# A router fed by halves: rows normed with one product ahead of the root, modulation rows stored dealt, and a reordered opening

## The reference

```
mod = silu(c) @ ada_w[l] + ada_b[l]      # 6 rows: sh1, sc1, g1, sh2, sc2, g2
h = rmsnorm(x, norm_mix_g[l]) * (1 + sc1) + sh1
x = x + g1 * mixer(h)                    # l=0: LRU and convolution; l=1: attention
h = rmsnorm(x, norm_ffn_g[l]) * (1 + sc2) + sh2
scores = sigmoid(h @ router_w)           # 16 experts in 4 groups, top group, top 2
x = x + g2 * sum_e gate_e * expert_e(h)  # silu(h wg) * (h wu) @ wd
out = rmsnorm(x, final_norm_g)           # latent tokens only
```

## Time and profile before

| | |
|---|---|
| time, median of 3 runs | 993.85 us (991.39 to 996.26) |
| the profiled execution's own time | 990.79 us |
| its span, first to last instruction | 989.0 us |
| PE busy | 907.5 us (92%) |
| DVE / ACT / POOL busy | 389.2 / 255.1 / 112.7 us |
| moved by DMA | 314.32 MB, mean 318 GB/s |
| chain that ended last | PE 61%, DMA 25%, DVE 8%, ACT 4%, issue 2% |

### The profile page before, as it was taken

The page is one execution under the profiler, slowest core; times in us unless marked ns, Lnnn a source line. Parts: engine busy times, 40 slices in busy tenths (PEclk is TensorE's granted clock), DMA queues, the critical chain, the costliest instruction groups (busy, mean ns, idle before and its releaser), DMA issues.

```text
span 989.0 us, 14182 instructions
## 1 busy us (share of the span) xinstructions
PE 907.5 (92%) x5142; PEld 473.8 (48%) x5143; DVE 389.2 (39%) x815; ACT 255.1 (26%) x393; POOL 112.7 (11%) x220
## 2 busy tenths in 40 slices
PE   3899999999779999999999959999966999999996
PEld 1433343344336656565656615458423545555453
DVE  1389989833662222222222252665153111111112
ACT  3423446412321122111111132155031111111112
POOL 2300000100021111111111120000002111111110
PEclk9999999999979999999999989999977999999999
DMA  9992496667598899989999993782636999999994
GB/s 351 347 362 85 181 342 242 244 226 276 185 359 328 317 420 425 421 313 419 382 428 422 391 331 122 259 318 84 254 128 234 395 402 406 419 425 426 421 425 195
DMA packets 68116, 314.32 MB, mean 318 GB/s; under 512 B 4516, under 2 KB 4884, under 8 KB 51696
## 3 DMA queue, kind: packets, MB, share of 16 engines
q1 hardware_dynamic: 54608, 275.78, 70.5%
q0 software_dynamic: 8800, 29.75, 8.2%
q10 hardware_dynamic: 4672, 8.30, 2.4%
HBM read 299.35 MB, written 14.47 MB: 317 GB/s over the span
## 4 chain that ended last, share of the span: by engine, by line
PE 61%; DMA 25%; DVE 8%; ACT 4%; issue 2%; ACTq 0%; SPq 0%; DVEq 0%
PE ps L764 17%; PE ps L777 9%; PE ps L566 9%; PE ps L602 6%; DMA weight_ring<-in_exp_w_down 5%; DMA weight_ring<-in_exp_w_up 4%; DMA weight_ring<-in_exp_w_gate 4%; PE ps L495 3%; PE ps L873 3%; PE ps L835 3%; DMA hT<-in_exp_w_down 2%; DMA arena<-in_exp_w_gate 2%; DMA arena<-in_exp_w_up 2%; DMA weight_ring<-in_ev_w_in 2%; DMA weight_ring<-in_ada_w 2%
## 5 line engine op out<-in xcount | busy, mean ns | idle before, releaser
L764 PE MATMUL ps<-weight_ring,arena 128*64 128x256 f32 x1792 | 201.2, 382 | 4.8 <-issue 3.3
L764 PEld LDWEIGHTS ps<-weight_ring,arena 128*64 128x64 f32 x1792 | 141.1, 138 | 72.3 <-issue 21.6
L1344 DVE TENSOR_TENSOR arena<-arena,ps 128x128 f32<-128x128 f32 x78 | 18.9, 285 | 255.9 <-PE ps L764 255.9
L566 PE MATMUL ps<-hT,weight_ring 128*128 128x512 f32 x256 | 113.6, 597 | 1.5 <-DMA weight_ring<-in_ev_w_in 0.9
L777 PE MATMUL ps<-weight_ring,arena 128*64 128x512 f32 x448 | 102.3, 597 | 2.6
L1062 DVE SCALAR_TENSOR_TENSOR arena<-arena,par 128x512 f32<-128x512 f32 x132 | 95.0, 749 | 5.5 <-PE ps L566 1.6
L1727 ACT ACT_TABLE_LOAD x39 | 50.0, 1283 | 129.6 <-issue 129.3
L566 PEld LDWEIGHTS ps<-hT,weight_ring 128*128 128x128 f32 x256 | 47.4, 190 | 64.8 <-issue 63.0
L764 PE MATMUL ps<-arena 128*64 128x256 f32 x704 | 78.0, 379 | 0.0
L602 PE MATMUL ps<-weight_ring,arena 128*128 128x512 f32 x160 | 70.8, 595 | 0.7 <-DVE arena L1494 0.5
L764 PEld LDWEIGHTS ps<-arena 128*64 128x64 f32 x704 | 56.3, 137 | 24.4 <-issue 5.9
(11 more groups left out here) (315 smaller groups left out, 914.6 us busy)
## 6 DMA issues: line engine op xcount, KB each, us to landing
weight_ring<-in_ada_w SPq DMA_DIRECT2D x24, 2048.0 KB, 15.0
weight_ring<-in_exp_w_gate SPq DMA_DIRECT2D x22, 2048.0 KB, 10.1
weight_ring<-in_exp_w_up SPq DMA_DIRECT2D x22, 2048.0 KB, 10.4
weight_ring<-in_exp_w_down SPq DMA_DIRECT2D x22, 2048.0 KB, 11.0
arena<-in_exp_w_gate SPq DMA_DIRECT2D x10, 2048.0 KB, 10.4
hT<-in_exp_w_down SPq DMA_DIRECT2D x10, 2048.0 KB, 10.6
arena<-in_exp_w_up SPq DMA_DIRECT2D x10, 2048.0 KB, 11.0
weight_ring<-in_ev_w_in SPq DMA_DIRECT2D x4, 2048.0 KB, 19.3
```

Source lines behind the costliest of these rows:

```text
L566: last = mm(ps[:, m % 4, :], wide(slot)[:, k, P * j:P * j + P], hT[:, k, :], start=(k == 0), stop=(k == KD - 1))
L764: last = mm(ps[64 * fh:64 * fh + 64, bank, 0:256], xgT[:, k % 4, 64 * (k // 4):64 * (k // 4) + 64], w[:, k, 256 * fh:256 * fh + 256], star ...
```

## The change

**Router.** The norm's two passes change places and are cut in column halves. `times_gain` multiplies x by the gain row first (it needs no root): its left half before the product of the pass c=1 is awaited, its right half when that half of x is ready. The second pass is one instruction for each half, h times the inverse root plus shift, and each half has its own count on `s_h`. ACT squares the left half early (`left_squares`), puts that sum into the root's bias, and in `moe_rms` squares only the right half. PE transposes and ACT copies by halves. The last tile's logits go to bank 3, and all transposes of partial sums come after them. The table for the sigmoid is loaded before the last tile's copies.

**Rows.** sh2 and sc2 are copied by ACT and stored by POOL dealt already, in runs of 16 elements (64 bytes): five stores in layer 0 instead of one, three in layer 1 instead of one.

**Opening.** The root's table is loaded early, the context tiles are squared when they land, DVE squares the last tile, the second ada chunk goes to bank 5, and the transposes of x stand between the ada products in smaller groups.

```diff
             def rows_transpose(l, i):
                 t = toks(l)[i]
-                pe.wait_ge(s_h[l], i + 1)
                 if i:
-                    pe.wait_ge(s_h2[l], i)
-                for k in range(KD):
-                    last = tr(ps[:, 4 + k // 4, P * (k % 4):P * (k % 4) + P], hrow[:, t - CT * l, P * k:P * k + P], ident[:, :])
-                last.then_inc(s_h2m[l], 1)
+                    pe.wait_ge(s_h2[l], 2 * i)
+                for hf in range(2):
+                    pe.wait_ge(s_h[l], 2 * i + hf + 1)
+                    for k in range(4 * hf, 4 * hf + 4):
+                        last = tr(ps[:, 4 + hf, P * (k % 4):P * (k % 4) + P], hrow[:, t - CT * l, P * k:P * k + P], ident[:, :])
+                    last.then_inc(s_h2m[l], 1)
...
-                logits(0, n - 1, 1)
+                logits(0, n - 1, 6, 0)
                 rows_transpose(l, n - 1)
-                logits(n - 1, n, 2)
+                logits(n - 1, n, 3, 0)
+                logit_columns(0, n - 1, 1)
+                logit_columns(n - 1, n, 2)
...
+                        if c:
+                            ahead_of(i)
                         dve.wait_ge(s_op[l], m + 1)
...
+            def times_gain(l, i, gain, hf):
+
+                t = toks(l)[i]
+                dve.wait_ge(s_res[l], len(toks(l)) * hf + i + 1)
+                mark(v.tensor_tensor(in_blocks(hrow[:, t - CT * l, :])[:, :, 64 * hf:64 * hf + 64],
+                                     by_rows(x[:, t, 512 * hf:512 * hf + 512]),
+                                     in_blocks((mb, mb1)[l][gain])[:, :, 64 * hf:64 * hf + 64], ALU.mult))
+
             def moe_norm(l, i, gain, shift):
-                if i == 0:
-                    dve.wait_ge(s_nr, 64 + 32 * l)
                 t = toks(l)[i]
+                times_gain(l, i, gain, 1)
                 invert(rstd[:, 2 + l, t:t + 1])
-                h = in_blocks(hrow[:, t - CT * l, :])
-                link(v.scalar_tensor_tensor(h, by_rows(x[:, t, :]), rstd[:, 2 + l, t:t + 1], by_rows((mb, mb1)[l][gain]), ALU.mult, ALU.mult))
-                v.tensor_tensor(h, h, by_rows((mb, mb1)[l][shift]), ALU.add).then_inc(s_h[l], 1)
+                for hf in range(2):
+                    h = hrow[:, t - CT * l, 512 * hf:512 * hf + 512]
+                    v.scalar_tensor_tensor(h, h, rstd[:, 2 + l, t:t + 1], (mb, mb1)[l][shift][:, 512 * hf:512 * hf + 512],
+                                           ALU.mult, ALU.add).then_inc(s_h[l], 1)
...
+            def left_squares(l, i):
+
+                t, row = toks(l)[i], 2 + l
+                act.wait_ge(s_res[l], i + 1)
+                if i:
+                    act.wait_ge(s_ss[1 + 2 * l], 3 * i)
+                s.activation(sq_row[l][:, 0:512], x[:, t, 0:512], ACT.Square,
+                             accum_out=ss[:, row, t:t + 1]).then_inc(s_ss[1 + 2 * l], 1)
+                act.wait_ge(s_ss[1 + 2 * l], 3 * i + 1)
+                s.activation(ss_left[:, l, t:t + 1], ss[:, row, t:t + 1], ACT.Identity, scale=1.0 / D,
+                             bias=epsc[:, 0:1]).then_inc(s_ss[1 + 2 * l], 1)
...
+                        left_squares(0, i)
+                        if i:
+                            rows_columns(0, i - 1)
                         moe_rms(0, i)
...
             def router(l):
                 n = len(toks(l))
+                s.activation(att[:, 3, 0:1], epsc[:, 0:1], ACT.Sigmoid)
+                rows_columns(l, n - 1)
...
-            g.dma_start(mod_dram[0][:, 0:3].rearrange("v i (k n) -> (i k) v n", n=P), mod_rows[0].rearrange("p (v n) -> p v n", v=2)).then_inc(s_mst, 16)
-            pool.wait_ge(s_mst, 16)
+            g.dma_start(mod_dram[0][:, 0].rearrange("v (k n) -> k v n", n=P),
+                        mod_rows[0][0:8, :].rearrange("p (v n) -> p v n", v=2)).then_inc(s_mst, 16)
+            for i in (1, 2):
+                for w in range(2):
+                    g.dma_start(mod_dram[0][w, i].rearrange("(c k a) -> k c a", c=KD, k=KD),
+                                mod_rows_dealt[0][8 * i:8 * i + 8, P * w:P * w + P].rearrange("p (c a) -> p c a", c=KD)).then_inc(s_mst, 16)
+            pool.wait_ge(s_mst, 80)
```

More of the change, by code:

```diff
@@ L542, in half_ready @@
                 pe.wait_ge(s_hTa[1] if pair % 2 else s_hTd[1], 4 * half + 2 * (pair // 2) + k % 2 + 1)
[L544 to L551, removed]
+            ada_product(6)
+            ada_columns()
+            ada_product(5)
+            param_transposes()
+            ada_columns()
+            xn_transposes(0, 3)
+            ada_product(6)
+            xn_transposes(3, 5)
+            ada_columns()
+            xn_transposes(5, 6)
+            ada_product(6)
+            ada_columns()
             xn_transposes(6, KD)
@@ L1147, in _, with add_residual @@
                                        ALU.mult, ALU.mult).then_inc(s_nrm, 1)
-            def add_residual(l, tiles, bc_of, after):
+            def add_residual(l, tiles, bc_of, ahead_of, after):
                 n_t = len(tiles)
@@ L1188, in after_residual, with ahead_of_residual @@
                     moe_norm(0, i, *((2, 3) if i < CT else (4, 5)))
-            add_residual(0, range(NT), lambda t: 0 if cond_of(t) == CON else 1, after_residual)
+            def ahead_of_residual(i):
+                if i == 0:
+                    dve.wait_ge(s_nr, 64)
+                times_gain(0, i, 2 if i < CT else 4, 0)
+            add_residual(0, range(NT), lambda t: 0 if cond_of(t) == CON else 1, ahead_of_residual, after_residual)
             link(add_bias(0, 10, 12))
@@ L1549, in rms @@
                 s.activation(out, src, ACT.Sqrt, scale=1.0 / n, bias=epsc[:, 0:1]).then_inc(s_rms, 1)
-            act.wait_ge(s_x, 32)
-            squares(0, 0, range(NT))
-            rms(rstd[:, 0, :], ss[:, 0, :], D, 0, NT)
+            s.activation(att[:, 3, 2:3], epsc[:, 0:1], ACT.Sqrt)
+            act.wait_ge(s_ctx, 16)
+            squares(0, 0, range(CT))
+            act.wait_ge(s_x, 16)
+            act.wait_ge(s_ss[0], CT)
+            s.activation(junk, x[:, CT, :], ACT.Square, accum_out=ss[:, 0, CT:CT + 1]).then_inc(s_ss[0], 1)
+            act.wait_ge(s_pc, 2)
+            rms(rstd[:, 0, :], ss[:, 0, :], D, 0, NT - 1)
             ada = [0]
@@ L1647, in mod_rows_read @@
                 act.wait_ge(s_modT, l + 1)
-                s.activation(mod_rows[l], ps[0:(24, 8, 24, 8)[l], bank, 0:(2 * P, 2 * P, P, P)[l]], ACT.Copy).then_inc(s_mrow, 1)
+                read = s.activation(mod_rows[l], ps[0:(24, 8, 24, 8)[l], bank, 0:(2 * P, 2 * P, P, P)[l]], ACT.Copy)
+                if l in mod_rows_dealt:
+                    read = s.activation(mod_rows_dealt[l].rearrange("p (v k a) -> p v k a", k=KD, a=16),
+                                        ps[0:24, bank, 0:(2 * P, 0, P)[l]].rearrange("p (v a k) -> p v k a", k=KD, a=16), ACT.Copy)
+                read.then_inc(s_mrow, 1)
             mod_rows_read(0, 5)
@@ L1817, in _ @@
             prob_columns(2 * HEADS - 1)
+            left_squares(1, 0)
             moe_rms(1, 0)
+            left_squares(1, 1)
             rows_columns(1, 0)
```

102 lines of the change are left out of this document (62 added, 40 removed).

## The result

The changed kernel took 979.08 us (median of 4 runs, 978.45 to 980.43), the kernel before 993.15 us beside it (median of 4, 991.39 to 996.26): ratio 0.9867, 95% interval 0.9846 to 0.9887. The profiled execution took 978.45 us, with a span of 976.6 against 989.0.

What follows compares the result with a forecast made beforehand. PE bounds layer 0's experts, DMA and PE are level in layer 1, and both pay for the router's delay of the first tile. Terms 5.7 + 7.5 + 0 + 0 = 13.2 us took 993.85 to 980.6 us; range 972.5 to 988.

Steps and rivals of the forecast that it cites:

- Layer 0's router: From layer 0's last residual to the routing: L1222 at 266.1 instead of 271.8, a gain of 5.7 us, between 4.8 and 6.3.
- Step 2: Layer 0's router, ACT: Square of 512 columns with its sum takes 0.70 us, to 261.5; root 0.29, to 261.8.
- Step 3: Layer 0's router, DVE: right gain product from 260.19 takes 1.0 us and ends at 261.2, ahead of the root.
- Step 4: Layer 0's router: reciprocal with gaps 0.22 us, then contiguous passes of 0.69 each; halves of h at 262.75 and 263.45.
- Step 5: Layer 0's router: four transposes take 0.55 to 0.8 us; sigmoid's table loaded by 263.3; copies end at 264.0 and 264.8.
- Layer 1's router: In layer 1, L1222 starts at 730.8 to 731.6 instead of 738.67: gain 7.1 to 7.9 us, taken as 7.5.
- the reasons for more: Rival, gain 16 to 19 us: third chunk lands sooner, or PE stays at 2.4 GHz in layer 1; chance 0.06.
- the prediction's cold bound: Layer 1's router, lower end of the gain: 7.1 us, with eight transposes at 1.97 us cold instead of 1.09 warm.
- Opening: First ev_w_in product up to 1 us sooner, but the third chunk still lands at 52.8: gain 0, from -0.5 to +1.
- Rows stored dealt: Layer 0's five stores of 64-byte runs take 6 us, hidden, as the residual needs the rows ten us after they land.
- the late gather: Rival, layer 0's first tile: packed weight loads delay the gather past some 2 us of slack; gain 8 to 11; chance 0.20, shared with cold PE.

Runs made afterwards that it cites:

- the two kernels with the same router and colder transposes: The changed kernel with POOL's 13 small loads after the first ev_w_in product, 978.04 us; the same with one layer-0 weight load behind the gather too, 974.54 us.
- gather first: The changed kernel with the 2 MB load of expert 1's down weights in layer 0 issued after the first tile's gathered rows land: 976.47 us, ratio 0.9842.
- router alone: The changed kernel without its opening, so router and dealt rows on the kernel before: 979.86 us, ratio 0.9878.
- both repairs: The changed kernel with one layer-0 weight load behind the first tile's gather and POOL's thirteen small loads after the first ev_w_in product: 974.54 us, ratio 0.9822.
- all five kernels with a part put back: The changed kernel with one undone: early gain product 984.49 us, halved transposes and copies 983.37, early table 979.97, dealt rows 981.96, halved squares 980.38.
- old opening with late loads: The changed router and dealt rows with the opening of the kernel before, POOL's thirteen small loads after the first ev_w_in product: 977.66 us, ratio 0.9852.
- small loads late: The changed kernel with POOL's 13 small loads issued after the first ev_w_in product instead of the first modulation: 978.04 us, ratio 0.9865.

## Why the prediction was right, step by step

**Forecast.** 980.6 us for a measured 979.1; by the profiled executions 13.2 us forecast and 12.34 measured (990.79 less 978.45), by the medians 14.1.

**Layer 0's router** (5.7): 6.33 at L1262, 0.45 of it brought along from the last residual, 5.88 in the chain itself. Step 2 took 0.70 for the Square and its sum: 0.63 and 0.20, which overlap, 0.76 up to the root. Step 3 took 1.0 for L1203: 1.10. Step 4 took 0.69 for each pass: 0.71. Step 5 had the table done at 263.3 and the first copy at 263.4; with the 0.45 by which the stage began sooner that is 262.85 and 262.95, and ACT was back at 262.78 and copied at 263.06, when PE's first half was done.

**Layer 1's router** (7.1 to 7.9, taken 7.5): 7.96 from the output projection to the routing. Tile 0 did not hold PE up any more, and PE stayed in part at the 2.4 GHz level, which the prediction had among the reasons for more. In the two kernels with the same router and colder transposes it is 7.1, the prediction's cold bound. Up to the first expert tile, with what stands ahead of the router, layer 1 gave 6.65: this term was 0.85 too large.

**Opening** (0, from -0.5 to +1): right in the changed kernel, which is 0.8 us faster by the medians than the one without it; alone it measured 1.2 us slower, outside that range. The reason given holds, since the third chunk landed at 53.03 for a predicted 52.8 though it was issued 1.2 us sooner. Chain of waits after:

```profile
33.48 19.55 DMA weight_ring<-in_ev_w_in
53.07 7.13 PE ps L577 x16
```

What the prediction did not name is what stood beside it in the engines: POOL's own loads, not the weight chunks ahead.

**Rows stored dealt** (hidden): right, though the prediction took the row loads' 7.8 us from three of the six; over all six it is 10.8 before and 10.6 after. In 178 to 202 us the stores and the row loads behind them (KB each, us to landing):

```profile
arena<-mod_rows POOLq DMA_DIRECT2D x6, 512.0 KB, 10.6
mod_rows<-arena POOLq DMA_DIRECT2D x4, 4.0 KB, 4.9
mod_rows<-arena POOLq DMA_DIRECT2D x1, 8.0 KB, 5.2
```

The stores of 4 KB in runs of 64 bytes landed in 4.9 us, where the prediction took 6, and the first residual of layer 0 waited for PE alone. The Trainium skill (DMA: Bandwidth & Descriptors, Specifications) asks for 512 bytes and more. The store of 8 KB beside them has runs of 512 bytes and landed in 5.2 us, so at a few KB no cost of the short runs shows here.

**The gather** was the step that failed in part. The sum counted the whole 5.7 us as passed on, with some 2 us of slack, and kept the late gather as a rival of 0.20. It was late: PE waited 3.40 us for it, and of the 5.88 us of the chain 1.21 were given back before the first tile; the run with the gather first shows the cause. The slack was not there: PE was done with the products ahead at 283.74 and needed 1.2 us more, and the gather landed at 287.10.

**What was not in the sum.** Layer 0 gave 5.88 less the 1.21 of the gather for the 5.7 forecast, layer 1 gave 6.65 for 7.5, together 11.3 for 13.2. The 12.4 of the spans are reached by 1.07 us in stages for which the sum had nothing (0.45 at the start, 0.12 and 0.5 in the experts). That these came on top is luck.

The part of layer 1 that needs explaining is the stage ahead of its output projection, which lost 2.07 us. There the changed kernel's PE ran, from the fourth ada product on (timeline, and clock of the stretch):

```profile
577.69 3.64 PE L498 MATMUL ps<-weight_ring,cond 128*32 128x512 f32 x16
587.92 3.67 PE L541 MATMUL ps<-ident,arena 128*128 128x128 f32 x16 [4.75 <-DVE arena L1422]
591.38 7.82 PE L855 MATMUL ps<-weight_ring,hT 128*128 128x512 f32 x16
```

```profile
578.00:592.00 14.00, 8.54 (x37) 4.92 (x30) 11.32 (x18) 7.59 (x15) 0.85 (x2) 0.50 0.82 295
```

In the kernel before the same three ran in 2.94, 3.32 and 7.03 us, at a clock of 0.69 in its stretch of 583 to 597 us for the 0.50 here. In all thirteen profiles (before, after, eleven experiments) this stage takes either 126.0 to 126.5 us (before, and seven of the experiments) or 127.9 to 128.3 (after, and four). Opening alone, router alone and gather first are among those of 128, both repairs and all five kernels with a part put back among those of 126. Each part of the change stands on both sides, so none of them by itself costs the 2 us.

Nor are the 2 us lost. Six kernels have the whole changed router. The four of them in the group of 128 (changed, router alone, gather first, old opening with late loads) have a granted clock of 0.50 there, and 0.83 to 1.00 in the 10 us that begin 28 us behind the start of the output projection; their router takes 35.25 to 35.63 us and the first tile starts 22.0 behind it. The two of 126 (small loads late, both repairs) have 0.64, then 0.74 and 0.73, and take 36.05 to 36.09 and 22.9 to 23.0. From the ada products to the first expert tile all six take 185.0 to 185.7 us, for 192.10 before. With the old router (opening alone) the 2 us stay: 194.7. PE waits there on others for much of the time; what decides the group, and why the clock behind it is the other way round, stays open.

## What to carry to other kernels

Between a row's statistics and its use, put every product that needs no root ahead of it, and split what is left in halves, so that VectorE, TensorE and ScalarE overlap: of the parts here these two were worth most, 2.9 and 1.7 us in layer 0 and some 2.7 and 2.3 in layer 1. Loading the sigmoid's table early was worth as much as the halves in layer 0 (1.7), but little of it reached the first tile. When a chain ahead of a gather gets shorter, look at what is issued in the time that it loses: large loads packed closer together made a gather of a few rows land 8.8 us after its issue, and one load moved behind it gave 1.4 us back at the next tile (2.6 by the medians, 1.0 by the spans). When a stage comes out slower for no instruction of its own, follow it to the next place where the engines meet before calling it a loss: here the 2 us were back by then. An opening made shorter is worth nothing while a transfer sets the next step; the small loads beside that transfer were the thing to move.

## What the runs showed that was not expected

- An operand at a step of 8 float32 elements costs VectorE 1.10 us for 512 columns instead of 0.71, and a second such operand in the same instruction costs nothing more (L1203, 1.10 with one, 1.11 with two).
- The same gather lands 3.6 us after its issue, or 8.8 behind three packed loads of 2 MB.
- DMA at a share of 1.05 moved 387 GB/s with weights alone, and 276 to 327 with POOL's small loads among them: the share says that the engines are busy, not what they deliver.
- In one stage with much waiting, PE's clock was 0.50 or 0.64 to 0.69, 2 us apart, in kernels that are alike there. Where it was 0.50 it was higher in the router that follows, and with the changed router the first expert tile started at the same distance in both.
